# Products into an unread PSUM bank, issued by TensorE ahead of its waits in prompt attention

## The reference, cut to what matters

```
s = einsum('bqngd,bqknd->bqngk', q, k_sel) * (HEAD_DIM ** -0.5) + bias
s = where((dist >= 0)[:, :, None, None, :], s, -inf)
p = softmax(s, axis=-1)
o = einsum('bqngk,bqknd->bqngd', p, v_sel)        # 16 heads, 4 key/value heads, 64 wide
```

## Time and profile before

| | us |
|---|---|
| runs, median of 3 | 3541.97 |
| profiled execution, its own time | 3546.85 |
| span of its trace | 3545.2 |
| prompt attention in it, first query scaling to last copy into mixT | 1144.27 to 1319.16 |

### The profile page before, as it was taken

One profiled execution on the slowest core, in us unless ns is written; L12 is line 12 of the kernel. 1 busy time (PEld: TensorE's weight loads), 2 busy tenths in 40 slices (PEclk: granted clock), 3 DMA queues, 4 the chain that ended last, 5 costly groups with the idle time before them and its releaser, 6 DMA issues. The chain is left out here.

```text
span 3545.2 us, 51907 instructions
## 1 busy us (share of the span) xinstructions
PE 3100.2 (87%) x21388; PEld 2826.0 (80%) x21388; DVE 1885.0 (53%) x3319; ACT 1032.4 (29%) x1195; POOL 108.4 (3%) x204
## 2 busy tenths in 40 slices
PE   3999749999934786586999999999999999999996
PEld 3999628888821332285999999999999999999995
DVE  3444256666555751144799888644444444444544
ACT  2222211111111110122444433333333433333332
POOL 0000000000003000000000000000000000000000
PEclk7999859898956557788999999999999999999998
DMA  2444200000015203341444444444445654444441
GB/s 112 159 154 154 97 6 10 19 10 20 10 35 146 114 30 114 122 169 72 168 159 161 164 158 156 172 167 167 164 162 193 206 195 167 163 162 165 165 167 63
DMA packets 106164, 442.77 MB, mean 125 GB/s; under 512 B 22697, under 2 KB 42770, under 8 KB 62562
## 3 DMA queue, kind: packets, MB, share of 16 engines
q1 hardware_dynamic: 93026, 399.98, 33.2%
q0 software_dynamic: 12928, 39.86, 3.4%
HBM read 422.11 MB, written 17.58 MB: 124 GB/s over the span
## 5 line engine op out<-in xcount | busy, mean ns | idle before, releaser
L2120 DVE TENSOR_TENSOR px_w_r<-px_w,px_wh 128x2048 fp32r<-128x2048 f32 x272 | 623.6, 2293 | 724.7 <-ACT px_wh L1956 724.1
L1956 ACT ACTIVATE px_wh<-px_w 128x2048 fp32r<-128x2048 f32 x272 | 521.3, 1917 | 1099.0 <-PE px_bank L255 602.7
L253 PE MATMUL px_bank<-pe_high,px_wh 128*128 128x288 f32 x2304 | 686.5, 298 | 26.2 <-DVE px_w_r L2120 26.2
L254 PE MATMUL px_bank<-pe_low,px_wh 128*128 128x288 f32 x2304 | 680.6, 295 | 0.0
L255 PE MATMUL px_bank<-pe_high,px_w_r 128*128 128x288 f32 x2304 | 678.1, 294 | 0.0
L253 PEld LDWEIGHTS px_bank<-pe_high,px_wh 128*128 128x128 f32 x2304 | 432.9, 188 | 26.7 <-issue 26.7
L255 PEld LDWEIGHTS px_bank<-pe_high,px_w_r 128*128 128x128 f32 x2304 | 434.9, 189 | 0.0
L254 PEld LDWEIGHTS px_bank<-pe_low,px_wh 128*128 128x128 f32 x2304 | 433.7, 188 | 0.0
L253 PE MATMUL px_bank<-px_arena_gh,px_wh 128*128 128x288 f32 x1024 | 303.3, 296 | 1.1 <-ACT px_h L1993 1.1
L253 PE MATMUL px_pair<-px_arena_gh,px_wh 128*128 128x288 f32 x1024 | 303.1, 296 | 0.0
L254 PE MATMUL px_bank<-px_arena_gl,px_wh 128*128 128x288 f32 x1024 | 302.1, 295 | 0.0
(11 more groups left out here) (424 smaller groups left out, 4868.4 us busy)
## 6 DMA issues: line engine op xcount, KB each, us to landing
px_w<-in_peer_u SPq DMA_DIRECT2D x128, 1024.0 KB, 4.9
px_w<-in_peer_v SPq DMA_DIRECT2D x128, 1024.0 KB, 4.8
in_w<-in_w_in SPq DMA_DIRECT2D x49, 1024.0 KB, 4.8
out_w<-in_w_o SPq DMA_DIRECT2D x16, 1024.0 KB, 4.8
px_w<-in_peer_wq SPq DMA_DIRECT2D x16, 1024.0 KB, 4.8
pq_pages<-in_kv_pages SPq DMA_DIRECT2D x48, 256.0 KB, 6.7
pq_pages<-in_kv_pages POOLq DMA_DIRECT2D x48, 256.0 KB, 5.8
g_rest<-px_rest POOLq DMA_DIRECT2D x36, 256.0 KB, 2.6
```

The source lines that it names most:

```text
L253: pe.matmul(out, w_high, high, start=start, stop=False, skip_group_check=True)
L254: pe.matmul(out, w_high, low, start=False, stop=False, skip_group_check=True)
L1956: act.activation(w_high[t % 2][:], w[t % SL][:], ACT.Copy).then_inc(raised, 1)
L2120: v.tensor_tensor(w_low[t % SL][:], w[t % SL][:], w_high[t % 2][:], ALU.subtract) \
```

## The change

TensorE's list gets a new helper, `idle_turns(count)`: it issues `count` products of `ident` (128x128) with 512 columns of the bias table `bias[1]` into `s_out`. Nobody reads them. It waits for nothing and raises nothing. It is called in three places: six products before the wait for `zeroed`, at the start of prompt attention; two at the head of chunks 1 to 5, after the wait for `staged` and before the first score; and one ahead of the wait for `normed` in each turn of chunks 0 to 5. That is 6 + 5 x 2 + 36 x 1 = 52 products. Chunks 6 and 7 are unchanged, and so are the lists of the other engines.

```diff
+                def idle_turns(count):
+
+                    for k in range(count):
+                        pe.matmul(s_out[:], ident[:], bias[1][:, 2 * k:2 * k + 2, :].rearrange("p a c -> p (a c)"),
+                                  start=True, stop=True)
+
                 def turn(n, u):
                     t, hf = units[u]
                     t0, m = QT_TILES[t]
+                    if n < 6:
+                        idle_turns(1)
                     pe.wait_ge(normed, n * U + u + 1)
...
+                idle_turns(6)
                 pe.wait_ge(zeroed, 2)
                 for n, (p, g) in enumerate(chunks):
                     pe.wait_ge(staged, n + 1)
+                    if n and n < 6:
+                        idle_turns(2)
                     for u in range(U + 2):
```

## The result

The changed kernel took 3546.61 us (median of 20 runs, 3540.71 to 3561.09), the kernel before 3540.76 us (20 runs, 3535.73 to 3548.32). The ratio is 1.0021, 95% interval 1.0013 to 1.003: slower by 5.9 us, about half of the forecast's +11.

A forecast was written before the change was run, and what follows sets the result against it. VectorE was taken to pace chunks 0 to 3 and TensorE chunks 4 and 5, with prompt attention's changes moving the kernel's end one for one. Terms +5.5 + 8.5 - 0.6 - 2.7 = +10.7 on 3541.97 gave 3553 us, range 3537 to 3565.

The forecast's parts named there:

- the tail of chunks 0 to 3: End of a VectorE-paced chunk: TensorE about 46% busy over 6.5 us, so the clock falls in most of them.
- the clock falls in fewer tails: Rival for chunks 1 to 3: one low start instead of two and a shorter low stretch; +5, 3547 us; chance 0.12.
- low start: A chunk of 1 to 3 beginning at the lower clock: 26.3 to 26.7 us against 22.9, +3.5 each; two counted.
- chunks 1 to 3 of 24 to 27 us, with 0.5 in the clock at their heads: Sign that the forecast is right: these chunk lengths, with the lower clock where the chunks begin.
- Six at the start: Start of prompt attention: six products take 8.1 to 9.1 us, first score 6.0 to 7.0 us late; chunk 0 +5.5 us.
- the price of a product: One added 512-column product, taken from L1702: 1.97 us at the lower clock, 1.05 us at the upper.
- Head pairs: Two products opening chunks 1 to 5, on the path in full: 2.1 us at the upper clock, 3.9 at the lower.
- Chunks 1 to 3: Two chunks beginning at the lower clock (+3.5 each), one beginning up and falling late (+1.4): +8.5 us.
- Chunks 4 and 5: TensorE paces without long gaps, so the clock should hold: 19.7 us each, -0.6 us for both.
- Chunk 6: No added products, inherits the upper clock; gains its first score and most lead-in steps before the fall: -2.7 us.
- One product a turn: Ahead of each turn: free while VectorE paces at the upper clock; at the lower, 2.3 us more per such step.
- The rival of a held clock: Clock holds from first rise through chunk 5 and beyond: -6.6 us, 3535 us, or 3541 if only to chunk 6; chance 0.20.

The follow-up runs named there:

- 32-partition run: The changed kernel with its 52 added products fed from 32 partitions instead of 128, still 512 columns: 3620.66 us in one run, +80 us against before.
- the kernel with six and tail pairs: The changed kernel without head pairs, two products per turn of units 4 and 5 in chunks 0 to 3: 3526.37 us, second time 3528.23 us.

## Why the prediction was right, and where a size was off

Its direction and its mechanism held: the added products act through the clock alone (the 32-partition run), the clock falls at the end of the tail of chunks 0 to 3 (TensorE busy 3.14 of the 6.50 us before, 48%; 46% was expected), and so the values of these chunks do not run at the upper clock while the head pairs lie on the path. Its sum, +10.7, was too large by 5 against the medians, and by 8 against the chunks of the trace.

The number itself is less good than the range makes it look. The measured 3546.61 us lies inside the 28 us of the range, but below the 3549.1 from which the prediction counted "slower" (0.66), in what it called "same" (0.25); with twenty runs of each kernel the interval does exclude no change. It is also almost to the microsecond the 3547 of the rival "the clock falls in fewer tails" (0.12). That agreement is chance: the rival had one low start, and the trace has none, with a tail that falls every time. The sign "chunks 1 to 3 of 24 to 27 us, with 0.5 in the clock at their heads" did not come: they took 23.9 and began up.

- **Six at the start.** Predicted 8.1 to 9.1 us for the six and +5.5 for chunk 0; measured 7.47 and +4.3. The mis-sized term is the price of a product. Several with the same weights in a row take 0.86 us each at the upper and 1.71 at the lower clock (the 36 single ones 0.96 and 1.86); the prediction had taken 1.05 and 1.97 from L1702, where each product stands alone.
- **Head pairs.** Predicted on the path in full, and so they are: 1.82 us at the upper clock (2.1 predicted), 3.57 at the lower (3.9).
- **Chunks 1 to 3.** Predicted +8.5, with two of three heads at the lower clock; the profiled execution had none and lost 3.05 us. The step that failed is the count of low starts: the clock came back during the values product each time, before the head. A low start, when it comes, costs what was predicted: 26.19 us in the kernel without the six (26.3 to 26.7). How often the changed kernel has one, no trace shows. The granted clock over the whole span is on record for each run: 0.916 in the profiled one, 0.915 in the ten from 3543.5 to 3546.8 us, 0.914 in the two near 3549, 0.912 or 0.913 in the five from 3551.2 to 3552.5, and 0.910 in the two above 3560. The trace of the kernel without the six, with its two low starts, reads 0.913. So the longer runs did spend more time at the lower clock, which fits low starts there; the median run needs none, if the rest of the kernel takes its usual time. That is argued, not shown.
- **Chunks 4 and 5.** Predicted 19.7 us each (-0.6 for both), measured 18.66 and 18.60 (-2.8). Again the price: six single products at 0.96 instead of 1.05 and a pair at 1.82 instead of 2.1 are 0.8 of the 1.1 us. That the clock held there was in the sum without a doubt attached; the low start of chunk 4 in the kernel without the six, 31.03 us, shows that it is not certain.
- **Chunk 6.** Predicted -2.7, measured -1.7. Chunk 7 as before, as predicted.
- **One product a turn.** Predicted to cost nothing while VectorE paces and the clock is up, and it did: in chunk 1 VectorE waits for the first score and the values alone.
- **The rival of a held clock** was wrong on this change: the clock fell in every tail of chunks 0 to 3. Its price for chunks 1 to 3, -0.2 us each, fits what was measured where the clock did hold (20.63 us, and a pair of 1.8 on top would make 22.4 to 22.5). Its -4.5 for chunk 6 and -5.3 for chunk 7 no run shows: in the second trace of the kernel with six and tail pairs the clock fell within chunk 6, and they gained 1.75 and 1.82 us. (The prediction's paragraph on the Trainium skill calls this the second rival; it is the first of its list.)

## What to carry to other kernels

Filler work for the clock belongs where the engine has slack and nothing else to do; here these were the last two steps of a chunk. Two products there, and none behind the wait that opens a chunk, turned +6 us into -13 to -15; the pairs behind that wait were nearly pure delay (9.3 us by the two kernels that differ in them alone). Look for the stretch in which the granted clock falls, not for the one in which the engine waits longest, and judge such a change by many runs: the one profiled execution was the best of twenty, and the same instructions took 25.78 us in one trace and 28.89 in another.

## What the runs showed of the hardware

- 512-column float32 products with 32 rows took the same time at the lower clock as with 128 rows: a pass 1056 ns against 1061, and the next one 0.85 us after it in both. With TensorE busy 33.16 of 34.20 us the clock stayed at 0.50; with 128 rows it came up within the first six products, 7.47 us.
- A busy TensorE did not by itself bring the clock back with 128 rows either: in chunk 4 of the kernel without the six it was busy 29.86 of 31.03 us, at a mean clock of 0.56. Why it came back at once elsewhere stays open.
- Runs of one kernel differed by up to 20 us (3540.71 to 3561.09, and 3524.14 to 3543.88 with the products at the turns alone), while the kernel before stayed within 13 us. In both the longer runs have the lower granted clock (0.910 against 0.916, and 0.910 against 0.915).
